# Attention stops of TensorE gathered at one place in every eight units: transposes, values and scores in a row, transposes in two PSUM banks, values in a projection bank

## What is computed

```python
for l in range(DEPTH):                       # DEPTH = 2
    h = _rmsnorm(x, norm_gain[l])
    proj = jnp.einsum('bsd,de->bse', h, w_in[l])            # 2048 -> 4352
    q, k, v, g_attn, x_rnn, g_rnn = jnp.split(proj, splits, axis=-1)
    attn = _swa_sink_attention(q, k, v, sinks[l], cos, sin)
    xc = _causal_conv(x_rnn, conv_w[l], conv_b[l])
    rnn = _rg_lru(xc, w_rgate[l], b_rgate[l], w_igate[l], b_igate[l], lru_param[l])
    mixed = jnp.concatenate([attn * jax.nn.silu(g_attn), rnn * jax.nn.silu(g_rnn)], axis=-1)
    x = x + jnp.einsum('bse,ed->bsd', mixed, w_out[l])      # 2048 -> 2048
return _rmsnorm(x, final_gain)

# in _swa_sink_attention: 16 query heads, 2 key/value heads of 64, chunks of 64 tokens,
# each chunk of queries sees its own and the chunk before it (128 keys)
logits = jnp.einsum('bcqkgd,bcjkd->bckgqj', qc, kb) * (HEAD_DIM ** -0.5)
probs = jax.nn.softmax(jnp.concatenate([logits, sink], axis=-1), axis=-1)[..., :-1]
out = jnp.einsum('bckgqj,bcjkd->bcqkgd', probs, vb)
```

## Time and profile before

| | |
|---|---|
| time, three runs | 2340.07, 2340.56, 2340.73 us; median 2340.56 |
| the profiled execution | 2340.98 us, of which the span of its instructions is 2339.2 us |
| busy, of the span | PE 2331.7 us (100%), PEld 1909.7 (82%), DVE 1387.5 (59%), ACT 1258.9 (54%) |
| chain of work that ended last | PE 99% |
| granted clock of TensorE | 0.999 |
| matmuls of the units (L410) | 9480, busy 2191.0 us |

### The profile page before, as it was taken

How to read it: one execution, slowest core, us unless ns; L and a number is a source line. 1 busy time by engine, 2 the same in 40 slices (tenths; PEclk the granted TensorE clock), 3 DMA queues, 4 the chain that set the end, 5 groups by cost and what they waited for, 6 DMA issues and landing times.

```text
span 2339.2 us, 31020 instructions
## 1 busy us (share of the span) xinstructions
PE 2331.7 (100%) x11466; PEld 1909.7 (82%) x11466; DVE 1387.5 (59%) x2238; ACT 1258.9 (54%) x2369; POOL 0.7 (0%) x7
## 2 busy tenths in 40 slices
PE   9999999999999999999999999999999999999999
PEld 7888888888888888888888888888888888888888
DVE  7557667435545767744475676764354467676335
ACT  7557666324455766634464576653244567665333
POOL 0000000000000000000000000000000000000000
PEclk9999999999999999999999999999999999999999
DMA  5334333333333223353334433233333332233334
GB/s 192 97 94 162 92 88 91 100 98 96 98 94 90 84 90 89 97 167 95 99 113 140 169 104 91 87 97 98 95 96 98 93 93 83 89 90 96 99 95 140
DMA packets 127016, 244.42 MB, mean 104 GB/s; under 512 B 14352, under 2 KB 18704, under 8 KB 126096
## 3 DMA queue, kind: packets, MB, share of 16 engines
q1 hardware_dynamic: 126288, 242.28, 33.7%
q10 hardware_dynamic: 576, 0.16, 0.0%
HBM read 234.00 MB, written 8.39 MB: 104 GB/s over the span
## 4 chain that ended last, share of the span: by engine, by line
PE 99%; DVE 0%; ACT 0%; issue 0%; POOL 0%; ACTq 0%; DVEq 0%; POOLq 0%
PE proj L410 92%; PE ps_sc L500 1%; PE ps_t L527 1%; PE ps_g L544 1%; PE ps_t L517 1%; PE proj L426 1%; PE proj L453 0%; PE ps_t L385 0%; DVE acc L998 0%; PE ps_t L484 0%; ACT operand L642 0%; DVE wcut L969 0%; ACT wcut L628 0%; PE ps_t L464 0%; PE proj L605 0%
## 5 line engine op out<-in xcount | busy, mean ns | idle before, releaser
L410 PE MATMUL proj<-operand,wcut 128*128 128x512 f32 x9480 | 2191.0, 391 | 0.1
L410 PEld LDWEIGHTS proj<-operand,wcut 128*128 128x128 f32 x9480 | 1772.3, 188 | 376.7 <-issue 7.0
L969 DVE TENSOR_TENSOR wcut<-wraw,wcut 128x512 fp32r<-128x512 f32 x804 | 554.9, 690 | 881.4 <-ACT wcut L628 878.2
L628 ACT ACTIVATE wcut<-wraw 128x512 fp32r<-128x512 f32 x803 | 506.5, 631 | 959.7 <-PE proj L410 942.5
L743 ACT ACTIVATE prob<-ps_sc,stat 128x128 f32<-128x128 f32 x256 | 90.2, 364 | 1.2
L711 ACT ACTIVATE gy<-proj 32x512 f32<-32x512 f32 x144 | 84.9, 589 | 3.8
L668 ACT ACTIVATE sqr<-x 128x512 f32<-128x512 f32 x62 | 36.8, 635 | 46.1 <-DVE x L1181 46.0
L998 DVE TENSOR_TENSOR acc<-acc,sqr 128x512 f32<-128x512 f32 x80 | 55.3, 691 | 4.9 <-ACT sqr L668 0.2
L743 ACT ACTIVATION_READ_ACCUMULATOR prob<-ps_sc,stat 128x1 f32 x256 | 52.0, 203 | 0.0
L1136 DVE SCALAR_TENSOR_TENSOR xc<-xr,pars,xc 128x512 f32<-128x512 f32 x64 | 48.1, 752 | 2.2
L980 DVE TENSOR_TENSOR operand<-mixed,operand 128x512 fp32r<-128x512 f32 x64 | 41.7, 688 | 10.3 <-ACT operand L650 9.6
(11 more groups left out here) (152 smaller groups left out, 1193.2 us busy)
## 6 DMA issues: line engine op xcount, KB each, us to landing
wraw<-in_w SPq DMA_DIRECT2D x804, 256.0 KB, 2.6
x<-in_xt SPq DMA_DIRECT2D x2, 4096.0 KB, 12.9
mixed<-in_xt SPq DMA_DIRECT2D x14, 512.0 KB, 6.9
gw<-in_gates SPq DMA_DIRECT2D x32, 128.0 KB, 2.6
out<-x SPq DMA_DIRECT2D x4, 1024.0 KB, 4.8
out<-mixed SPq DMA_DIRECT2D x7, 512.0 KB, 3.4
tab<-in_cossin SPq DMA_DIRECT2D x8, 256.0 KB, 3.2
mixed<-in_xt SPq DMA_DIRECT2D x4, 256.0 KB, 4.0
```

The costliest lines, as they stand in the source:

```text
L410: last = pe.matmul(bank[:, :], wcut[:, u % RING, a, c:c + P], operand[:, k, b, :], start=(k == 0 and n == 0), stop=(k == KT - 1 and n == 2))
L628: act.activation(wcut[:, u % RING, 0, :], wraw[:, u % RING, :], ACT.Copy).then_inc(w_hi, 1)
L969: dve.tensor_tensor(wcut[:, u % RING, 1, :], wraw[:, u % RING, :], wcut[:, u % RING, 0, :].bitcast(F32), ALU.subtract).then_inc(w_lo, 1)
```

## The change

All of it is in the order and the place of the attention work; no operation is added or dropped.

- `VISIT` becomes 36 + 8p: 36, 44, 52, 60, 68, 76, 84, 92, 100, 108. Every visit stands in the fifth unit of a group.
- `prob_transposes` does all eight transposes at slot `VISIT[p+1]` itself (before +2 and +4), the first four into `ps_t`, the second four into `ps_g`, the bank of the recurrence's gates. Behind them in the same stop come `values` of the visit before and `scores` of the next.
- `values` writes into bank 0 of the pair of projection banks whose group has been finished (`value_bank`) and waits for that bank's evacuation; the next group's last wait now covers `attn_done` too. `gate` waits for the copies of the transposes.
- The second `exponent` goes from V+6 to V+5; both `prob_copy` go to V+1 (before +3 and +5). `softmax_norm` stays at V+7.
- `v_transposes` does all eight at slot 18.
- G1, the slots of `gated`, moves for two tiles from 78, 79 to 80, 81.

```diff
-VISIT = [31 + 78 * p // 9 for p in range(NP + 2)]
+VISIT = [36 + UPG * p for p in range(NP + 2)]
...
+        ps_tr = [ps_t[:, :, :], ps_g[:, :].rearrange("p (a b) -> p a b", a=TPK)]
...
+        def value_bank(l, p):
+
+            g = VISIT[p + 2] // UPG
+            return bank_of(l, 2 * g - 2)[:, :].rearrange("p (i t b) -> p i t b", i=2, t=TPK)
...
                                 pe.wait_ge(evac, h * (DEPTH * TILES) + (l * TILES + 2 * STREAM[s + 1][0] + 2))
+                                for p in range(NP):
+                                    if VISIT[p + 2] // UPG == s // UPG:
+                                        pe.wait_ge(attn_done, per_layer(h, l, NP, p + 1))
...
+            def prob_transposes(h, l, p):
+
+                pe.wait_ge(p_done, per_layer(h, l, NP, p + 1))
+                if p > 0:
+                    pe.wait_ge(pt_done, per_layer(h, l, NB, 2 * p))
                 else:
-                    pe.wait_ge(pt_done, per_layer(h, l, NB, 2 * p + 1))
...
+                gates_read = sum(r + 7 < VISIT[p + 1] for r in R0)
+                if gates_read:
+                    pe.wait_ge(i_done, per_layer(h, l, 2 * RT, 2 * gates_read))
+                for i in range(2):
+                    for odd in range(2):
+                        for pair in range(2):
+                            last = pe.transpose(ps_tr[i][:, 2 * odd + pair, :], prob[:, odd, i, pair, :], idn[:, :])
+                    last.then_inc(t_done, 1)
...
                 pe.wait_ge(pt_done, per_layer(h, l, NB, 2 * p + 2))
+                pe.wait_ge(evac, at_evac(h, l, 2 * (VISIT[p + 2] // UPG) - 2))
+                ps_v = value_bank(l, p)
...
+                    copied = sum(v < R0[j] + 5 for v in VISIT[1:NP + 1])
+                    pe.wait_ge(pt_done, per_layer(h, l, NB, 2 * copied))
...
                         for p in range(NP):
-                            for i in range(2):
-                                if s == VISIT[p + 1] + 2 + 2 * i:
-                                    prob_transposes(h, l, p, i)
+                            if s == VISIT[p + 1]:
+                                prob_transposes(h, l, p)
...
                             for i in range(2):
-                                if s == VISIT[p] + 4 + 2 * i:
+                                if s == VISIT[p] + 4 + i:
                                     exponent(h, l, p, i)
```

More of the change, by code:

```diff
@@ L162, in build @@
         ps_t = ctx.enter_context(nc.psum_tensor("ps_t", [P, TPK, P], F32))
-        ps_v = ps_t[:, :, :].rearrange("p (i a) (m b) -> p i (a m) b", i=2, m=2)
         ps_g = ctx.enter_context(nc.psum_tensor("ps_g", [P, TOK], F32))
+        ps_tr = [ps_t[:, :, :], ps_g[:, :].rearrange("p (a b) -> p a b", a=TPK)]
         ps_tok = ps_t[:, 0:3, 0:HT // P]
@@ L472, in split_sum_of_squares, with v_transposes @@
                 last.then_inc(ss_done, 1)
[L474 to L485, removed]
+            def v_transposes(h, l):
+                pe.wait_ge(k_done, per_layer(h, l, 5, 5))
+                pe.wait_ge(cross_done, per_layer(h, l, 2, 2))
+                pe.wait_ge(evac, at_evac(h, l, EV_V))
+                for i in range(2):
+                    for c in range(4):
+                        t0 = CH * (4 * i + c)
+                        last = pe.transpose(ps_tr[i][:, c, :], vfeat[:, t0:t0 + P], idn[:, :])
+                    last.then_inc(vt_done, 1)
             def scores(h, l, p):
@@ L503, in scores @@
                 last.then_inc(s_done, 1)
[L505 to L512, removed]
-                else:
-                    pe.wait_ge(pt_done, per_layer(h, l, NB, 2 * p + 1))
[L515 to L518, removed]
+            def prob_transposes(h, l, p):
+                pe.wait_ge(p_done, per_layer(h, l, NP, p + 1))
+                if p > 0:
+                    pe.wait_ge(pt_done, per_layer(h, l, NB, 2 * p))
+                else:
+                    pe.wait_ge(vtok_done, per_layer(h, l, 2, 2))
+                gates_read = sum(r + 7 < VISIT[p + 1] for r in R0)
+                if gates_read:
+                    pe.wait_ge(i_done, per_layer(h, l, 2 * RT, 2 * gates_read))
+                for i in range(2):
+                    for odd in range(2):
+                        for pair in range(2):
+                            last = pe.transpose(ps_tr[i][:, 2 * odd + pair, :], prob[:, odd, i, pair, :], idn[:, :])
+                    last.then_inc(t_done, 1)
             def values(h, l, p):
@@ L561, in _ @@
                             split_sum_of_squares(h, l)
-                        if s in (VT_TR, VT_TR + 2):
-                            v_transposes(h, l, (s - VT_TR) // 2)
+                        if s == VT_TR:
+                            v_transposes(h, l)
                         for p in range(NP):
-                            for i in range(2):
-                                if s == VISIT[p + 1] + 2 + 2 * i:
-                                    prob_transposes(h, l, p, i)
+                            if s == VISIT[p + 1]:
+                                prob_transposes(h, l, p)
+                        for p in range(NP):
                             if s == VISIT[p + 2]:
@@ L723, in v_copy @@
                 act.wait_ge(vt_done, per_layer(h, l, 2, i + 1) + 1)
-                act.activation(vtok[:, 4 * i:4 * i + 4, :], ps_t[:, :, :], ACT.Copy, scale=0.5).then_inc(vtok_done, 1)
+                act.activation(vtok[:, 4 * i:4 * i + 4, :], ps_tr[i], ACT.Copy, scale=0.5).then_inc(vtok_done, 1)
             def gate_tanh(h, l, n):
@@ L751, in prob_copy @@
                     act.wait_ge(v_done, per_layer(h, l, NP, p))
-                act.activation(probT[:, :, i, :, :], ps_t[:, :, :].rearrange("p (o a) b -> p o a b", o=2),
+                act.activation(probT[:, :, i, :, :], ps_tr[i].rearrange("p (o a) b -> p o a b", o=2),
                                ACT.Copy).then_inc(pt_done, 1)
@@ L759, in attn_out @@
                 to = mixed[:, TPK * kv:TPK * kv + TPK, CH * c:CH * c + 2 * CH].rearrange("p t (i b) -> p i t b", i=2)
-                act.activation(to, ps_v, ACT.Copy).then_inc(attn_done, 1)
+                act.activation(to, value_bank(l, p), ACT.Copy).then_inc(attn_done, 1)
             def gate_weights_hi(h, l, j):
@@ L842, in _ @@
                             for i in range(2):
-                                if s == VISIT[p + 1] + 3 + 2 * i:
+                                if s == VISIT[p + 1] + 1:
                                     prob_copy(h, l, p, i)
@@ L884, in _ @@
                             shift(h, l, t + 1, tile_of("q", t))
-                        if s in (VT_TR + 1, VT_TR + 3):
-                            v_copy(h, l, (s - VT_TR - 1) // 2)
+                        if s == VT_TR + 1:
+                            for i in range(2):
+                                v_copy(h, l, i)
                         if s - 3 in R0:
```

## The result

The changed kernel takes 2350.58 us (median of 5 runs, 2350.41 to 2351.23), against 2340.56 us before (median of 5 runs beside it, 2340.07 to 2341.11): 10.0 us more, a ratio of 1.0044 with a 95% interval of 1.0032 to 1.0055. It is slower, by not quite three quarters of the 13.7 us that were forecast, and inside the range.

A forecast was written before the change was run, and what follows sets the result against it. TensorE bounds the kernel, 99% of the chain of waits. Waits for the division 15.6 us less 1.9 for joined stops gave +13.7 us, 2354.3 us against a median of 2340.56; range 2346.5 to 2361, about 8 in 10.

The forecast's parts named there:

- the three visits named: Visits 2, 4 and 7: TensorE's transposes wait for VectorE's division, 0.89, 1.50 and 1.50 us, in every pass.
- The size of the waits: TensorE's waits for the division: 3.89 us a pass, 15.6 us over four passes.
- the joined stops: TensorE: 48 fewer stops, each saving 0.03 to 0.05 us, 1.9 us in all (bounds 1.4 and 2.4).
- The end of the division: VectorE, visit 4: `p_done` at 14.83 us after the start of unit 72; the transposes' weight load due at about 13.38.
- The price of a whole joined stop: TensorE: transposes, values and scores in one stop cost about 0.88 + 2.30 = 3.2 us.
- The visits in time: Division early enough: visit 3 by 0.43 us, visit 5 by nearly 1, visits 0, 1 and 6 by more.
- the rival without a drain: Values or scores behind transposes start without the 0.11 us delay: another 3.1 us over 28 stops; with division in time, 2335.6.
- What was counted as free: Second transpose bank, values in the projection bank with its evacuation and `attn_out` waits, `gate` waiting for copies: no cost.
- the division is in time after all: VectorE slots V+5 to V+7, visits 2, 4, 7: no wait, -1.9 us, 2338.7 us; chance 0.08.
- the waits are smaller: Waits smaller or fewer, as ScalarE makes up its delay: about +4 to +8 us, 2345 to 2348; chance 0.09.
- The clock rival: TensorE's clock falls in the 12 waits, one unit each at half speed: +33 us more, 2387; chance 0.03.
- the rival of dearer stops: TensorE: stops save more than 0.05 us each; no total and no chance of its own given.

The follow-up runs named there:

- norm_slot6: Changed kernel with softmax_norm one slot earlier, at V+6 instead of V+7: 2339.41 us; repeats 2338.80 and 2338.84 us.
- split_stop: Changed kernel with softmax_norm at V+6, first behind weight_lo, and the eight transposes one unit earlier as a stop of their own: 2345.90 us.
- more_work: Changed kernel with one more VectorE instruction in slot V+6 of each visit, a maximum over 128x512 that nobody reads: 2358.31 us.
- exp_back: Changed kernel with the second half of the exponentials back at V+6 instead of V+5: 2351.74 us.
- norm_first: Changed kernel with softmax_norm still in V+7 but first behind weight_lo, ahead of lru_m2 and gate_weights_lo: 2340.91 us.

## Why the prediction was right, point by point

**The bound and the mechanism.** TensorE's stream with no slack, a division pushed to the end of VectorE's slot V+7, transposes that ask for it two units after the start of that slot: all as forecast, in the three visits named and in no other. The experiments move the cost as the mechanism says: 11.4 us gone with the division early, 0.94 a wait for 0.95 us of work moved behind it, 0.37 for ScalarE's 0.37, 0.6 for 0.6 added.

**The size of the waits** was too large, 15.6 us summed against 11.4 measured; with the joined stops, 1.6 for 1.9, that makes the 9.8 of the stretch out of the 13.7. Two terms of the waits were mis-sized.

- The end of the division. In visits 4 and 7 it was summed at 14.83 and came at 14.71. ScalarE starts the first exponential 0.11 us after the small operation on `stat` (804.78 to 804.89), where the earlier trace rows had 0.24. That row is of visit 5, though the prediction says that its durations are those of the same slots. In visit 4 itself the kernel before had 0.11 too, behind a load of a table of functions:

```profile
791.88 1.28 ACT L737 ACT_TABLE_LOAD   x1
793.18 0.21 ACT L737 ACTIVATE stat<-stat 128x8 f32<-128x8 f32 x1
793.29 0.35 ACT L743 ACTIVATE prob<-ps_sc,stat 128x128 f32<-128x128 f32 x1
```

The prediction had no term for that load. In the changed kernel it comes two slots earlier (798.01), with idle time of 1.35 us behind it on ScalarE; ahead of the exponentials it would have added up to 1.28 us. That it could be left out was luck. In visit 2 the sum was a further 0.12 high: it took off `gated` at 0.61, but `silu` ahead of it also gets shorter, from its start to the next 0.60 in visit 2 (first pair) in place of the 0.72 of visit 4 (second pair):

```profile
760.59 0.68 DVE L1094 SCALAR_TENSOR_TENSOR mixed<-gt,mixed 128x512 f32<-128x512 f32 x1
761.19 0.69 DVE L981 TENSOR_TENSOR wcut<-wraw,wcut 128x512 fp32r<-128x512 f32 x1
...
812.93 0.68 DVE L1094 SCALAR_TENSOR_TENSOR gy<-gt,gy 128x512 f32<-128x512 f32 x1
813.65 0.69 DVE L1106 TENSOR_TENSOR mixed<-mixed,gy 128x512 f32<-128x512 f32 x1
```

In idle weight loading all this makes 13.7 instead of 15.6.
- What such a wait costs. I charged the whole idle time of the weight load. But the load runs 0.22 us ahead of its matmul, in time in which the last matmul is still streaming. A load that has waited is followed by its matmul almost at once (both at 817.64), so most of that lead is no loss: 1.17 for 1.39, and 0.45 for the 0.66 of visit 2, 2.3 us over twelve waits. The idle time on PE's own row, 8.7 in all, is too small a measure in turn; the price, 11.4, lies between the two rows.

**The joined stops** were given 1.9 us. Pair by pair beside the kernel before, the version without waits gains 1.2, 1.6 and 1.6 us; each interval includes no change, all three medians lie on one side. By the stretch it gains 1.61 (2248.38 - 2246.77), 0.4 in each pass: 0.034 for each of the 48 stops, and 0.05 on the pair that differs in nothing but 28 stops and the place of the division within a slot. The bounds of 0.03 and 0.05 hold; 0.04 for every stop was a little high. The price of a whole joined stop was said to be 3.2 us. In norm_slot6 it is 3.02 from the transposes to the next unit (812.84 to 815.86) and 0.14 more in that unit, which takes 2.86 (to the gates at 818.72): 3.16.

**The visits in time.** Visit 3 was summed at 0.43 to spare and has 0.59 (0.64 less the 0.05 from VectorE to the load), visit 5 at nearly 1 and has 1.09. Visit 0 was put among those that are in time "by more", without a sum. It has 0.5, in the third pass nothing. In this visit ScalarE also shifts a query tile and loads a table, and in the third pass VectorE scales the output as well. That no wait came of it was luck; split_stop and more_work showed it. One count is off as well: 32 stops, not 28, have values or scores behind transposes, so the rival without a drain was worth 3.5 us and not 3.1.

**What was counted as free** was free: no wait at the second PSUM bank, at the evacuated projection bank or at `attn_done`, and TensorE's granted clock did not fall, neither around the wait nor over the span, where it is 0.999 as before (windows; PE, PEld, DVE, ACT, POOL busy, then the clock):

```profile
802.00:817.00 15.00, 14.68 (x65) 11.78 (x63) 11.18 (x20) 12.95 (x33) 0.00 (x0) 1.00 0.30 87
817.00:833.00 16.00, 15.36 (x102) 12.30 (x103) 11.78 (x19) 9.90 (x21) 0.00 (x0) 1.00 0.29 85
```

**The rivals.** That the division is in time after all fell: it was 1.4 us late. Its price, though, is what norm_slot6 shows, 2338.8 to 2339.4 against the 2338.7 given. That the waits are smaller came true in part, for the two reasons above. The clock rival and the rival of dearer stops fell.

## What to carry to other kernels

Engines that are busy for 59% and 53% of the span set the time of a kernel that is bound by TensorE as soon as an exchange between them has less room than the local backlog: before moving a consumer earlier, add up what its producer has queued in the slots ahead, engine by engine, in the units of the engine that is the bound. A stop less is worth 0.03 to 0.05 us here and a missed exchange 0.4 to 1.2 us, so a rearrangement that saves stops has to leave the producers their room; moving the division one slot earlier together with the transposes gave the small gain without the loss. And check the visits that are in time, too: two of the surprises here (visit 3 in exp_back, visit 0 in split_stop) were visits with about half a microsecond to spare, one of them never summed.

## What the runs showed of the hardware that was not expected

- A waiting weight load costs TensorE less than its idle time. The unit behind comes later by 0.20 to 0.21 us less than the load was idle: 1.18 for 1.39, 0.45 for 0.66, 0.30 for 0.50 (exp_back), 0.25 for 0.45 (norm_first). That is nearly the 0.22 us by which loads otherwise run ahead of their matmul.
- The distance from a small operation (128x8) to the first exponential on ScalarE is not fixed but takes one of two values. In the kernel before it is 0.12 us in visits 1 to 4 and 6 and 0.23 in visits 0, 5 and 7, the same in all four passes; in the changed kernel it is 0.12 in all but visit 0. What decides it is open. VectorE's 4.11 and 3.22 us of a slot repeated to 0.01 in the changed kernel.
- Values (another shape of the array) start 0.09 us late behind transposes (0.53 less 0.44), about as late as behind a unit, where 0.11 was read. The Trainium skill (TensorEngine Tiling (Array Packing), Key Properties) has changing the tiling mode drain TensorE; the trace agrees in that the values start late. No run separates a drain from another cause of the 0.09.
